# First norm over GpSimd's products, silus one turn later, and the delta rule five ticks earlier

## The chip, the cores and the metric

The kernel runs on one core of one Trainium2 chip, whose engines work side by side: TensorE (PE, with PEld for its weight loads), VectorE (DVE), ScalarE (ACT), GpSimd (POOL) and SyncE (SP), which issues the loads. The metric is the device time of one execution in microseconds (us). Less is better.

## The reference, cut to what matters

Two transformer blocks run one after the other on 512 tokens of width 1024. The change lies in the first block, from its start to the end of its input projection.

```python
c_act = jax.nn.silu(c)
mod = (c_act @ w_ada[l] + b_ada[l])[:, None, :]
shift1, scale1, gate1, shift2, scale2, gate2 = jnp.split(mod, 6, axis=-1)
h = rms_norm(x, norm1_w[l]) * (1.0 + scale1) + shift1
# in hybrid_mixer(h, ...)
p = h @ w_in
qkv = jax.nn.silu(causal_depthwise_conv(p[..., Q_OFF:Z_OFF], conv_qkv_w))
...
o = gated_delta_rule_chunked(l2_normalize(q), l2_normalize(k), v, g, beta)
```

The delta rule takes 64 tokens at a time: from q, k, v and the decays it inverts a triangular 64x64 matrix for each chunk and head, and then carries a 128x128 state for each head from chunk to chunk.

## The kernel before

Everything is held with the features on the 128 partitions: X is 8 tiles of 128x512 (KT = 8). Each engine has a program of its own (`tensor`, `vector`, `scalar`, `gpsimd`, `sync`). The order on an engine is the order in which its Python function is written, and semaphores join the engines.

**The norm.** ScalarE squares X tile by tile (L1679), GpSimd adds six of the squares (L2186), TensorE sums over the partitions with a matrix of ones (`sum_squares`, L518 and L521), and ScalarE makes the reciprocal root RSTD by Ln and Exp (`rstd`, L1694 and L1696). Meanwhile the first two of the six parts of the modulation (shift1 and scale1) are formed from 16 slabs of w_ada in the buffer ADA: of each part TensorE multiplies two slabs (`ada_direct`, L542) and VectorE weighs and adds six (`weigh`, L1053 and L1056), which TensorE then sums (`ada_column`, L533). `apply_norm` (L1082, L1075) on VectorE and `upper` (L1721) on ScalarE write the normed X as a high part HH and a low part HL.

**The matmuls.** Each weight slab of 128x1024 is loaded into one of four buffers RAWS (L2350). ScalarE rounds it into WH (`split_to`, L1666), GpSimd forms the rest WL in four pieces of 128x256 (L2169), and TensorE multiplies in eight k steps of three matmuls each (`slab_gemm`, L498). There are three WH and three WL, so WH of a slab waits for the matmul of the slab three before. `begin(which, j, 1)` splits up to one slab beyond the named one. The first slab, `ab` (512 wide, for the decays), runs in alternation with the first slab of w_in. I call the slabs of w_in w0 to w27, in their order.

**Slabs w0 to w11** are q, k and v. They end in one of two PSUM banks, in turn. ScalarE reads a bank twice (`evict`: STG at L1745, TMP at L1747), VectorE adds three taps of the convolution (`convolve`, L1140), and ScalarE applies the silu (`silu`, L1752), for q and k also the square (L1755). TensorE sums the squares of four heads at a time (`l2_sums`, L572), ScalarE forms the roots (`l2_roots`, L1761 and L1764), and VectorE scales the heads (`unit_heads`, L1147). Between them VectorE weighs one further slab of w_ada per turn. The loads of w_in and of w_ada alternate in one queue of SyncE: a w_ada slab waits for the buffer that VectorE's weighing two w_ada slabs earlier frees, and the w_in slab behind it in the queue waits with it.

**Slabs w10 to w27 and the delta rule** are woven: each engine alternates the stream `project_rest` (two ticks, and again two) with the stream of the delta rule (two ticks, and then three). A k step of TensorE is one tick, a slab is eight. The delta stream begins after DELTA_TICKS empty ticks. In it two prepared pairs of chunks and one scan take turns. `prepare` begins with two broadcasts of the decays and of beta (L680, L684, 8 matmuls each in the profile), then k and q products, transposes (kq, tr) and the inversion (L615, L634); `scan` carries the state (L738 to L751).

## Time and profile before

| | us |
|---|---|
| median of 3 runs | 2103.99 (2103.61 to 2108.41) |
| profiled execution | 2104.05 |
| its span | 2102.8 |
| PE busy | 1945.7 (93%) |
| PEld busy | 1657.3 (79%) |
| DVE busy | 680.6 (32%) |
| ACT busy | 710.3 (34%) |
| POOL busy | 950.0 (45%) |
| mean granted clock | 0.963 |

The table is of the whole span. The change touches the first 385 us only, so the shares of busy time say little; what counts there is where TensorE stands still, which instruction ends each wait, and which clock it was granted. Busy times of TensorE are modelled, since matmuls are pipelined: a matmul of 128x512 starts 0.23 us after the one before at the higher clock. The row that the timeline gives after idle time names the engine and line that released it; "issue" stands where the profile shows no releaser, and then the semaphore that the program waits on has to be found in the other engines' rows.

### The profile page before, as it was taken

The page shows a single profiled execution, that of the slowest core. Times are in us where ns is not written, and L with a number is a line of the kernel's source. Part 1 is how long each engine was busy: PE and PEld are TensorE (multiplying, and loading weights), DVE is VectorE, ACT ScalarE, POOL GpSimd, SP SyncE. Part 2 cuts the span into 40 slices and gives each one's busy share as a digit, 9 for nine tenths or more (in the row PEclk, how much of TensorE's full clock was granted, in tenths as well). Part 3 has the DMA queues.
Part 4 walks back from the last instruction along what each step waited for, and adds up shares of the span by engine and source line. Part 5 has one row for each costly group of instructions (what it writes and reads, how often), then busy time and mean ns, then how long its engine had stood idle before and what let it go on. Part 6 is the DMA issues. An engine that isn't in the chain of part 4 may idle for free.

```text
span 2102.8 us, 32887 instructions
## 1 busy us (share of the span) xinstructions
PE 1945.7 (93%) x13928; PEld 1657.3 (79%) x13928; DVE 680.6 (32%) x1069; ACT 710.3 (34%) x1093; POOL 950.0 (45%) x1257
## 2 busy tenths in 40 slices
PE   5879989999999999999999999977777799999997
PEld 4657767777788889999999989966666478888885
DVE  6554452232111102232210055654454522222101
ACT  3573221332232234222222243444455343222222
POOL 3442231535545566555555455421122166555564
PEclk8999998999999999999999999998999899999998
DMA  7332121324332233222222422100000323322231
GB/s 279 120 123 98 68 94 32 102 73 146 120 101 88 90 96 97 91 91 91 89 83 94 131 88 86 45 7 2 2 2 2 130 80 101 92 99 91 92 101 58
DMA packets 54690, 182.75 MB, mean 87 GB/s; under 512 B 6512, under 2 KB 6768, under 8 KB 54416
## 3 DMA queue, kind: packets, MB, share of 16 engines
q1 hardware_dynamic: 54544, 180.65, 26.1%
q8 instruction: 110, 1.80, 0.3%
q14 instruction: 36, 0.29, 0.0%
HBM read 175.39 MB, written 5.24 MB: 86 GB/s over the span
## 4 chain that ended last, share of the span: by engine, by line
PE 81%; DVE 7%; ACT 6%; DMA 3%; issue 2%; POOL 1%; SPq 1%; DVEq 0%; ACTq 0%
PE PS L498 67%; PE PS L615 3%; PE PS L969 1%; DVE TMP L1140 1%; DMA ADA<-w_ada 1%; PE PS L962 1%; POOL WL L2169 1%; ACT WH L1666 1%; PE PS L976 1%; PE PS L987 1%; DMA BON<-bsave 1%; DMA RAWS<-w_f0g 1%; ACT L1673 0%; PE PS L744 0%; PE PS L748 0%
## 5 line engine op out<-in xcount | busy, mean ns | idle before, releaser
L2169 POOL TENSOR_TENSOR WL<-RAWS,WH 128x256 fp32r<-128x256 f32 x1074 | 822.2, 797 | 809.8 <-ACT WH L1666 809.7
L498 PE MATMUL PS<-HH,WH 128*128 128x264 f32 (+2 forms) x2184 | 670.7, 349 | 47.3 <-issue 10.6
L498 PE MATMUL PS<-HL,WH 128*128 128x264 f32 (+2 forms) x2184 | 656.1, 342 | 0.0
L498 PE MATMUL PS<-HH,WL 128*128 128x264 f32 (+2 forms) x2184 | 654.1, 341 | 0.0
L498 PEld LDWEIGHTS PS<-HH,WH 128*128 128x128 f32 (+1 forms) x2184 | 378.3, 191 | 114.8 <-issue 31.5
L1666 ACT ACTIVATE WH<-RAWS 128x1024 fp32r<-128x1024 f32 (+2 forms) x275 | 283.7, 1033 | 457.5 <-PE PS L498 401.9
L498 PEld LDWEIGHTS PS<-HH,WL 128*128 128x128 f32 (+1 forms) x2184 | 378.8, 191 | 48.8 <-issue 0.6
L498 PEld LDWEIGHTS PS<-HL,WH 128*128 128x128 f32 (+1 forms) x2184 | 379.0, 190 | 48.0 <-issue 2.6
L498 PE MATMUL PS<-IHf,WH 128*128 128x512 f32 (+1 forms) x704 | 209.4, 338 | 0.0
L498 PE MATMUL PS<-IHf,WL 128*128 128x512 f32 (+1 forms) x704 | 209.2, 338 | 0.0
L498 PE MATMUL PS<-ILf,WH 128*128 128x512 f32 (+1 forms) x704 | 209.2, 338 | 0.0
L1401 DVE TENSOR_TENSOR TMP<-TMP,PS 128x512 f32<-128x512 f32 (+1 forms) x66 | 45.8, 693 | 322.9 <-PE PS L498 308.0
L1944 ACT ACTIVATE IHf<-TMP 128x512 fp32r<-128x512 f32 (+1 forms) x66 | 42.0, 636 | 286.5 <-DVE TMP L1401 286.5
L498 PEld LDWEIGHTS PS<-IHf,WH 128*128 128x128 f32 x704 | 120.6, 188 | 14.9
L498 PEld LDWEIGHTS PS<-ILf,WH 128*128 128x128 f32 x704 | 120.7, 188 | 14.7
L498 PEld LDWEIGHTS PS<-IHf,WL 128*128 128x128 f32 x704 | 120.4, 188 | 14.9
L1408 DVE SCALAR_TENSOR_TENSOR X<-PS,X 128x528 f32<-128x528 f32 (+1 forms) x16 | 11.2, 700 | 222.5 <-PE PS L498 222.5
L2186 POOL TENSOR_TENSOR SQA<-SQA,TMP 128x512 f32<-128x512 f32 (+1 forms) x39 | 53.1, 1363 | 63.2 <-ACT TMP L1679 62.5
L1389 DVE TENSOR_TENSOR TMP<-PS,RSTD 128x528 f32<-128x528 f32 (+1 forms) x44 | 30.8, 700 | 151.1 <-PE PS L498 150.4
L1403 DVE TENSOR_TENSOR ILf<-TMP,IHf 128x512 fp32r<-128x512 f32 (+1 forms) x66 | 46.8, 709 | 46.4 <-ACT IHf L1944 46.4
L1679 ACT ACTIVATE TMP<-X 128x512 f32<-128x512 f32 (+1 forms) x42 | 26.1, 626 | 85.8 <-DVE X L1408 35.7
L1396 DVE TENSOR_TENSOR TMP<-TMP,RSTD 128x528 f32<-128x528 f32 (+1 forms) x44 | 36.7, 833 | 41.3 <-ACT TMP L1940 41.3
(498 smaller groups left out, 1810.7 us busy)
## 6 DMA issues: line engine op xcount, KB each, us to landing
RAWS<-w_w_in SPq DMA_DIRECT2D x52, 512.0 KB, 4.3
RAWS<-w_ada SPq DMA_DIRECT2D x32, 512.0 KB, 3.6
RAWS<-w_f0g SPq DMA_DIRECT2D x22, 512.0 KB, 3.5
RAWS<-w_f0u SPq DMA_DIRECT2D x22, 512.0 KB, 3.6
RAWS<-w_f1g SPq DMA_DIRECT2D x22, 512.0 KB, 3.5
RAWS<-w_f1u SPq DMA_DIRECT2D x22, 512.0 KB, 3.5
RAWS<-w_f2g SPq DMA_DIRECT2D x22, 512.0 KB, 3.5
RAWS<-w_f2u SPq DMA_DIRECT2D x22, 512.0 KB, 3.5
```

Of the source, the lines that this page charges most:

```text
L498: ins = te.matmul(ps[0:m, q, o:o + b - a] if len(halves) > 1 else ps[0:m, o:o + b - a], w[:, k * m:k * m + m], v[:, k0 + k, a:b], start=fi ...
L615: ins = te.matmul(h4(b[:, 0:256])[q, u, :], lhs[q, u, :], con("ident")[q, q] if rhs is None else rhs[q, u, :], start=True, stop=True)
L962: te.matmul(PS[:, b, 0:n], KA[q, i, 128 * j:128 * j + 128], QA[q, i, 512 - n:512], start=True, stop=True).then_inc(*hp[b].up("z", r))
L1389: ve.tensor_tensor(tv, place(f, 2 * j), r, ALU.mult).then_inc(*ff_g.up("g", FT * (f - 1) + j))
L1396: ve.tensor_tensor(tv, tv, r, ALU.mult).then_inc(*ff_g.up("r", FT * (f - 1) + j))
L1401: ve.tensor_tensor(tv, tv, place(f, 2 * j + 1), ALU.mult).then_inc(*ff_mul.up(FT * f + j))
L1403: ve.tensor_tensor(IL[f][:, j, :], t, IH[f][:, j, :].bitcast(f32), ALU.subtract).then_inc(*ff_lo.up(FT * f + j))
L1666: ae.activation(WH[s % NS][:, 0:n], RAW[i % NR][:, 0:n], ACT.Copy).then_inc(*w_hi.up(s))
L1679: ae.activation((TMP[k % 3] if k else SQA)[:, 0:n], X[:, k, t0:T2], ACT.Square).then_inc(*n_sq.up(8 * SQUARED[q] + k))
L1944: ae.activation(IH[f][:, j, :], t, ACT.Copy).then_inc(*ff_hi.up(FT * f + j))
L2169: ins = ge.tensor_tensor(WL[s % NS][:, p], RAW[i % NR][:, p], WH[s % NS][:, p].bitcast(f32), ALU.subtract)
L2186: ge.tensor_tensor(SQA[:, 0:n], SQA[:, 0:n], TMP[k % 3][:, 0:n], ALU.add).then_inc(*n_acc.up(added(q, k)[1] - 1))
```

## The change

It has three parts.

1. GpSimd multiplies each tile of X by RSTD into a new buffer XRS, which lies behind ADA in memory that later tensors use. ScalarE forms HH from XRS in one instruction with scale SC and shift MOD, and VectorE forms the same value in TMP with `tensor_scalar` and subtracts HH. On TensorE the sum of squares moves between the two `ada_direct`. On GpSimd the memset of ST, which lies over XRS, moves behind the splits of w0 to w11 and waits for the last HL.
2. On ScalarE `silu(i - 1)` in the turn of slab i becomes `silu(i - 2)`, and so on to slab 12, where `log_and_exp` (which loads the table with Exp and Ln) now follows silu(11).
3. DELTA_TICKS goes from 30 to 25 on all four engines.

```diff
-DELTA_TICKS = 30
+DELTA_TICKS = 25
...
         te.wait_ge(*c_act.at("silu"))
-        for v in range(2):
-            ada_direct(v, bank(v))
+        ada_direct(0, bank(0))
         te.wait_ge(s_k0, 16)
         sum_squares(0)
+        ada_direct(1, bank(1))
...
-        apply_norm(0, SC[:, 0:8], MOD[:, 0:8], NM)
+        def first_low(k):
+            ve.wait_ge(*n_h.at(k))
+            ve.wait_ge(*n_hi.at(k))
+            ve.tensor_tensor(HL[:, k, NM:T2], TMP[k % 3][:, 0:T1], HH[:, k, NM:T2].bitcast(f32),
+                             ALU.subtract).then_inc(*n_lo.up(k))
+
+        for k in range(KT):
+            ve.wait_ge(*n_xr.at(k))
+            if k >= 3:
+                ve.wait_ge(*n_lo.at(k - 3))
+            ve.tensor_scalar(TMP[k % 3][:, 0:T1], XR[k], SC[:, k:k + 1], MOD[:, k:k + 1], ALU.mult,
+                             ALU.add).then_inc(*n_h.up(k))
+            if k:
+                first_low(k - 1)
+        first_low(KT - 1)
...
-        upper(0, MOD[:, 0:8], NM)
+        ae.wait_ge(*s_sc.at(0))
+        for k in range(KT):
+            ae.wait_ge(*n_xr.at(k))
+            ae.activation(HH[:, k, NM:T2], XR[k], ACT.Identity, bias=MOD[:, k:k + 1],
+                          scale=SC[:, k:k + 1]).then_inc(*n_hi.up(k))
...
-            silu(i - 1)
+            if i > 1:
+                silu(i - 2)
...
         evict(9)
+        silu(8)
         begin("w_in", IN_ORDER[11], 1)
         l2_roots(4)
-        silu(9)
...
-                if 10 < i < 13:
-                    silu(i - 1)
                 for _ in range(8):
                     yield
                 if i < 12:
                     evict(i)
+                    silu(i - 1)
                     continue
...
+                    if i == 12:
+                        silu(11)
+                        log_and_exp()
...
         pr, dr = project_rest(), later_by(DELTA_TICKS, pipeline(4, prepare, scan))
-        log_and_exp()
...
+        ge.wait_ge(*n_rs.at("r0"))
+        for k in range(KT):
+            ge.tensor_tensor(XR[k], X[:, k, NM:T2], RSTD[:, 0:T1], ALU.mult).then_inc(*n_xr.up(k))
         ge.wait_ge(*ada_col.at(1))
         for i in range(2):
             ge.memset(STG[i][:, 0:3], 0.0).then_inc(*zeros.up(f"stg{i}"))
         ge.memset(ROW[:, :], 0.0).then_inc(*zeros.up("row"))
+        begin("w_in", IN_ORDER[10], 1)
+        ge.wait_ge(*n_lo.at(7))
         ge.memset(ST[:, :, :], 0.0).then_inc(*zeros.up("st"))
-        begin("w_in", IN_ORDER[10], 1)
```

GpSimd's queue at the start, before: the additions of squares, memsets, and the WL pieces.

```order
7 L2186 TENSOR_TENSOR SQA<-SQA,TMP 128x512 x6
8 L2194 MEMSET STG 128x3 x2
9 L2195 MEMSET ROW 64x512
10 L2196 MEMSET ST 128x512
11 L2169 TENSOR_TENSOR WL<-RAWS,WH 128x256 x66
```

GpSimd's queue at the start, after:

```order
7 L2210 TENSOR_TENSOR SQA<-SQA,TMP 128x512 x6
8 L2218 TENSOR_TENSOR XRS<-X,RSTD 128x512 x8
9 L2221 MEMSET STG 128x3 x2
10 L2222 MEMSET ROW 64x512
11 L2193 TENSOR_TENSOR WL<-RAWS,WH 128x256 x50
12 L2225 MEMSET ST 128x512
```

Eight products stand ahead of the memsets and of every WL piece, and the memset of ST stands behind 50 pieces.

ScalarE's queue after the roots of heads 4 to 7 (X<-X), up to the first instruction of the delta rule (L1861 before, L1886 after), before:

```order
76 L1764 ACTIVATE X<-X 128x512 x4
77 L1752 ACT_TABLE_LOAD
78 L1752 ACTIVATE QKV<-TMP 128x512
79 L1673 ACT_TABLE_LOAD
80 L1745 ACTIVATE STG<-PS 128x512
81 L1747 ACTIVATE TMP<-PS,CV 128x512
82 L1752 ACT_TABLE_LOAD
83 L1752 ACTIVATE QKV<-TMP 128x512
84 L1745 ACTIVATE STG<-PS 128x512
85 L1747 ACTIVATE TMP<-PS,CV 128x512
86 L1666 ACTIVATE WH<-RAWS 128x1024
87 L1752 ACTIVATE QKV<-TMP 128x512
```

and after:

```order
76 L1786 ACTIVATE X<-X 128x512 x4
77 L1767 ACTIVATE STG<-PS 128x512
78 L1769 ACTIVATE TMP<-PS,CV 128x512
79 L1774 ACT_TABLE_LOAD
80 L1774 ACTIVATE QKV<-TMP 128x512
81 L1767 ACTIVATE STG<-PS 128x512
82 L1769 ACTIVATE TMP<-PS,CV 128x512
83 L1774 ACTIVATE QKV<-TMP 128x512
84 L1684 ACTIVATE WH<-RAWS 128x1024
85 L1886 ACT_TABLE_LOAD
86 L1886 ACTIVATE X<-PS 128x512
87 L1830 ACTIVATE Z<-PS 128x512
```

The eviction of w10 (STG, TMP) stands directly behind the roots, and EG of the delta rule (X<-PS) stands ahead of the eviction of w12 (Z).

TensorE's queue around the second broadcasts of the delta rule, before (w13, k steps 2 and 3 between the two):

```order
350 L680 MATMUL PS<-ROW,KC 128x128 x4
351 L684 MATMUL PS<-ROW,KC 128x128 x4
352 L498 MATMUL PS<-HH,WH 128x512
353 L498 MATMUL PS<-HL,WH 128x512
354 L498 MATMUL PS<-HH,WL 128x512
355 L498 MATMUL PS<-HH,WH 128x512
356 L498 MATMUL PS<-HL,WH 128x512
357 L498 MATMUL PS<-HH,WL 128x512
358 L680 MATMUL PS<-ROW,KC 128x128 x4
359 L684 MATMUL PS<-ROW,KC 128x128 x4
```

and after (w12, k steps 6 and 7 between the two):

```order
339 L684 MATMUL PS<-ROW,KC 128x128 x4
340 L688 MATMUL PS<-ROW,KC 128x128 x4
341 L502 MATMUL PS<-HH,WH 128x512
342 L502 MATMUL PS<-HL,WH 128x512
343 L502 MATMUL PS<-HH,WL 128x512
344 L502 MATMUL PS<-HH,WH 128x512
345 L502 MATMUL PS<-HL,WH 128x512
346 L502 MATMUL PS<-HH,WL 128x512
347 L684 MATMUL PS<-ROW,KC 128x128 x4
348 L688 MATMUL PS<-ROW,KC 128x128 x4
```

The broadcasts moved ahead by four k steps, 12 matmuls of the projection.

## Rows read from the trace of the kernel before

**Rows 1.** The page, part 2: tenths in 40 slices of 52.6 us.
```profile
PE   5879989999999999999999999977777799999997
...
PEclk8999998999999999999999999998999899999998
```

**Rows 2.** Timeline, 18 to 46 us: start, duration, engine, line, tiles, count, idle before.
```profile
18.06 6.87 DVE L1056 SCALAR_TENSOR_TENSOR ACC<-ADA,CA,ACC 128x1024 f32<-128x1024 f32 x4 [1.79 <-DMA ADA<-w_ada]
...
23.20 6.99 PE L542 MATMUL PS<-CA,ADA 128*128 128x1 f32 x32 [1.42 <-DMA ADA<-w_ada]
...
28.30 5.53 DVE L1056 SCALAR_TENSOR_TENSOR ACC<-ADA,CA,ACC 128x1024 f32<-128x1024 f32 x4 [0.39 <-DMA ADA<-w_ada]
...
33.77 0.69 ACT L1694 ACTIVATE RSTD<-PS,EPSC 128x512 f32<-128x512 f32 x1 [14.22 <-PE PS L521]
...
34.49 0.63 ACT L1696 ACTIVATE RSTD<-RSTD 128x512 f32<-128x512 f32 x1
...
44.83 0.80 PE L498 MATMUL PS<-HH,WH 128*128 128x512 f32 x1 [2.39 <-POOL WL L2169]
```

**Rows 3.** Timeline of GpSimd, additions, memsets and WL pieces.
```profile
10.83 10.18 POOL L2186 TENSOR_TENSOR SQA<-SQA,TMP 128x512 f32<-128x512 f32 x6 [9.94 <-ACT TMP L1679]
...
37.38 0.14 POOL L2194 MEMSET STG<- 128x3 f32 x2 [16.37 <-PE PS L533]
...
38.38 6.39 POOL L2169 TENSOR_TENSOR WL<-RAWS,WH 128x256 fp32r<-128x256 f32 x6
```

**Rows 4.** Timeline of TensorE, projection: instructions after idle time.
```profile
60.61 0.57 PE L498 MATMUL PS<-HH,WH 128*128 128x512 f32 x1 [2.46 <-issue]
...
75.60 0.47 PE L498 MATMUL PS<-HH,WH 128*128 128x512 f32 x1 [1.64 <-issue]
...
82.22 0.47 PE L498 MATMUL PS<-HH,WH 128*128 128x512 f32 x1 [0.83 <-issue]
...
120.69 0.79 PE L498 MATMUL PS<-HH,WH 128*128 128x512 f32 x1 [4.63 <-ACT TMP L1747]
...
147.31 0.50 PE L498 MATMUL PS<-HH,WH 128*128 128x512 f32 x1 [2.13 <-ACT TMP L1747]
...
157.23 0.76 PE L498 MATMUL PS<-HH,WH 128*128 128x512 f32 x1 [4.05 <-issue]
```

**Rows 5.** Tile SQA, 10 to 30 us: ns shortest, median, longest.
```profile
L2186 POOL TENSOR_TENSOR SQA<-SQA,TMP x6: 1262/1398/2065, 10.8 to 18.9; 128x512 f32<-128x512 f32 x6
```

**Rows 6.** Timeline of ScalarE and the load queue: turns of the loop.
```profile
77.28 1.04 ACT L1666 ACTIVATE WH<-RAWS 128x1024 fp32r<-128x1024 f32 x1
...
82.69 0.63 ACT L1752 ACTIVATE QKV<-TMP 128x512 f32<-128x512 f32 x1 [3.31 <-DVE TMP L1140]
...
83.90 1.04 ACT L1666 ACTIVATE WH<-RAWS 128x1024 fp32r<-128x1024 f32 x1
...
105.65 0.43 SPq L2350 DMA_DIRECT2D RAWS<-w_w_in  x1
...
110.11 1.06 ACT L1666 ACTIVATE WH<-RAWS 128x1024 fp32r<-128x1024 f32 x1 [2.71 <-DMA RAWS<-w_w_in]
```

**Rows 7.** Windows of TensorE: us, busy (instructions), granted clock, DMA share, GB/s.
```profile
83.00:87.60 4.60, 4.60 (x21) 1.00 0.46 154
...
160.00:165.00 5.00, 5.00 (x20) 0.50 0.10 38
...
352.00:376.00 24.00, 22.44 (x84) 0.57 0.13 43
```

**Rows 8.** Timeline of ScalarE after the two groups of roots.
```profile
119.48 0.58 ACT L1745 ACTIVATE STG<-PS 128x512 f32<-128x512 f32 x1
...
144.79 1.28 ACT L1673 ACT_TABLE_LOAD   x1
```

**Rows 9.** Timeline of TensorE in the delta rule.
```profile
167.62 1.05 PE L684 MATMUL PS<-ROW,KC 64*128 64x128 f32 x8
...
301.62 0.68 PE L615 MATMUL PS<-iv1LD,iv1UD 64*64 64x64 f32 x16 [2.93 <-DVE iv1LD L1234]
```

More of the change, by code:

```diff
@@ L203, in program @@
     ADA = sbuf("ADA", [128, 16, SLAB], st=m0)
+    XRS = sbuf("XRS", [128, KT * T1], st=m0)
     m0.close()
@@ L330, in program @@
     n_res, n_pre, n_outp = count("n_res"), count("n_pre"), count("n_outp")
+    n_xr = count("n_xr")
     ff_silu, ff_mul, ff_hi, ff_lo, ff_x = (count(x) for x in ("ff_silu", "ff_mul", "ff_hi", "ff_lo", "ff_x"))
@@ L446, in place @@
         return pair((job + 2) % 3) if f == 1 else bank(job % 6)
+    XR = [XRS[:, 512 * k:512 * k + 512] for k in range(KT)]
     NORMED = {0: 0, 1: 1, 3: 2, 4: 3, 5: 4}
```

## The prediction

> **What bounds the kernel now.** I read the page's 40 slices first [rows 1]: TensorE is busy 9 tenths nearly everywhere until 1425 us, but not in the first three slices (0 to 158 us). Between TensorE's instructions the kernel is nearly saturated, so a gain can only come from time in which TensorE stands still or runs at the lower of its two clocks (0.50 granted is 1.2 GHz, 1.00 is 2.4 GHz). All three parts of the change lie before 385 us, where the input projection ends. There the timeline shows where TensorE stood: for the conditioning at the start [rows 2], for GpSimd's low halves of the weights [rows 3], and at eight places in the projection, of which six stand in [rows 4]. Everything after 385 us follows in order and should only slide. The profiled execution took 2104.05 us (span 2102.8), the median of the three runs is 2103.99, so I count from 2104.05.
>
> **Part 1, the start.** Before, TensorE waits 1.42 us for the second half of w_ada, multiplies until 30.2, sums the squares until 33.7, and ends the columns at 37.3, which releases GpSimd [rows 2, 3]. After, the sums of squares (3.7 us) stand between the two halves: 21.8 to 25.5; the second half runs to 32.5 and the first eight columns to 34.4, with no idle time. The reciprocal root, 0.69 + 0.63 us on ScalarE, is ready at 26.9 instead of 35.1 [rows 2]. That alone would end the columns 1.1 us sooner.
>
> But the first projection's pair of slabs does not wait for the norm: its first matmul at 44.83 is released by GpSimd's WL [rows 2], and from there TensorE has no other wait until 60.61 [rows 4], so none for a norm tile. The bound is GpSimd's queue: memsets from 37.4, then six WL pieces in 6.39 us [rows 3]. The change puts eight products of 128x512 ahead of those. No row has them there. The nearest are the six additions of the same size: shortest 1.26, longest 2.07 us, six in 10.18 [rows 3, 5]. They are long where VectorE works beside them, and VectorE is then slowed too: four weighings take 6.87 us with GpSimd busy for the first half, 5.53 with it idle [rows 2].
> The Trainium skill has a rule that speaks against this edit (SBUF — State Buffer, section Who interferes with whom): a VectorE instruction with two SBUF inputs contends with a GpSimd instruction that reads SBUF, and one of them blocks for the whole of the other. Taken to the letter a product beside a weighing would cost 1.26 + 1.28 = 2.5 us and the pair would start near 53, for a sum of 2095. The longest row, 2.07, has not shown that much.
>
> I take 1.87 us for a product while VectorE is busy and 1.3 otherwise. VectorE's last four weighings then take 4 x 1.9 from 28.3, until 35.9; by then 4.8 products are done. The second eight columns wait for that weighing: 36.0 to 37.8, SC at 38.1. By then 6.5 products are done; the rest takes 2.7 us beside VectorE, to 40.9. Memsets 0.6 (the one of ST, 0.5, is moved away) and six WL at 1.1 give 48.1. So the pair starts **3.3 us later** than at 44.83. Bounds: all products at 1.26 from 26.95 on and WL as before, -0.4 us; all at 2.07 and WL at 1.14, +6.1. VectorE's and ScalarE's cheaper norm (the products are taken from them) is worth nothing here, since HL was not waited for. The clock is low at the pair's start in both kernels, since TensorE stands still before it in both.
>
> **Part 2, the silus, slabs 1 to 9.** One turn of ScalarE's loop is WH at 77.28, two evictions, a wait of 3.3 us for VectorE's three taps, silu and square, WH at 83.90: 6.62 us [rows 6]. Then WL takes 3.7 and TensorE starts: idle 0.83 at 82.22 (three such places) and 1.64 at 75.60 [rows 4]. A slab needs only 24 x 0.23 = 5.55 us (20 starts in 4.6 us; the row counts one more, under way [rows 7]). With silu(i-2) the wait for taps is gone. What is late next is the DMA: the load of w(n+3) is queued behind an ada slab that waits for VectorE's weighing of slab n, itself behind the taps; issued at 105.65 it lets ScalarE start at 110.11, 4.45 us later [rows 6]. I walk it on, in the times of before (evictions 1.15, taps 3.2, weighing 1.3, WH 1.05, WL done 3.85 after it). WH of w3 67.0, WL done 71.9: w3 starts at 73.96, idle 0. Load of w4 lands at 75.5, WL done 80.4: w4 at 80.45. Then w5 86.0, the l2 sums 91.6 to 95.3, w6 95.3, w7 100.85, w8 106.4.
> The roots: the load of w9 lands at 103.6 (before: 110.11); WH, table, four Ln, four Exp, silu, square are 9.4 us from WH's start to the next eviction at 119.48 [rows 6, 8], plus 1.15: 114.2. So **w9 starts at 114.2 instead of 120.69**, after 2.2 us idle instead of 4.63 [rows 4], and I take it that it then stays at 2.4 GHz (a wait of 2.13 at 147.31 left it there; one of 2.46 at 60.61 did not). If it falls, 12 matmuls x 0.2 = 2.4 us come back; I charge half, 1.2.
>
> **Part 3, slabs 10 to 13.** w10 waits for the eviction of w9, which stands behind WH of w11, whose load waits for VectorE after the w9 start (taps, unit heads, weighing, landing: 11 us): 127.0 instead of 133.5. w12 waits for the eviction of w10. Before, this one stood behind two table loads of 1.28 and a silu of 0.63 after the roots, 3.3 us with the gaps, the last ending at 146.07 [rows 6, 8]; after, it stands directly behind the roots. WH of w12 at 129.1 makes the roots end at 136.0 and the eviction at 137.15, before w11 ends at 138.1. **w12 starts at 138.1, not 147.31.** Inside w12 now stand the first broadcasts of the delta rule, 2.2 us at 2.4 GHz. The second ones end at 148.05. w13's load lands at 143.1 and its WL at 148.0: no idle time, where before there were 4.05 us and after them the lower clock (0.50 from 160 to 165) [rows 4, 7]. One common point: both broadcasts and four steps of w13 done. Before this is 168.7 (the second broadcasts end at 167.62 + 1.05 [rows 9]); after, 148.05 + 4 x 3 x 0.23 = 150.8. **That is 17.9 us sooner**, start excluded.
> The added table loads (Exp for EG inside w12, Silu and back for silu(11)) put WH of w14 at 149.9 and its WL at 154; TensorE has work until 160.9. They cost nothing; without the two kq pieces and the transposes, 7.2 us, as cover they would.
>
> **Part 4, the weaving itself.** The delta rule stands four k steps, 2.8 us, earlier in TensorE's order from there on, and 12 projection matmuls more follow its last sum. Busy work is equal, so only waits and clock count. Before has single waits for VectorE, the longest 2.93 us at 301.62 [rows 9], where the short convolution sits in VectorE's queue, and 24 us at the end with a clock of 0.57 [rows 7], which is 22.44 x 0.43 = 9.6 us of lost work. The shift redraws them and nothing says which way: I take 0, bounds -8 (most of the slow end and one wait gone) to +8 (as much again). Of the end, the wait of 0.20 for the last gated part goes; the 1.60 for the short convolution stays.
>
> **The sum.** +3.3 - 17.9 + 1.2 - 0.2 + 0 = -13.6, so 2104.05 - 13.6 = **2090.5 us**.
>
> **Rivals.** (a) *The start is free and the delta stretch falls well.* VectorE's weighing does not hold GpSimd back: -0.4 instead of +3.3, and the slow end shrinks by 5: about 2082. For it: the shortest addition took 1.26; against: four of six were far longer. (b) *The loads bind.* My walk leaves w4 to w9 within 1 us of the DMA. If each landing is 1 us later (the 4.45 is one row), the evictions of w7 and w9 come 3 us later each, and a fall of the clock at w9 and w13 costs 2.4 + 3.7: with that the gain is 13.6 - 9 = 4.5: 2099.5. (c) *The silus move nothing*: something else, such as the evictions of TMP for a later slab, holds TensorE as before; then only w12's 3.3 us and w13's wait stay, less the start: 2104 - 4 = 2100 or more, counted as the same. Against it: each of these waits ends in a WL or an eviction that I traced to ScalarE's queue. (d) *Slower*: the delta rule in its new place meets VectorE's taps so that TensorE stays at 1.2 GHz through it. It would have to lose 13.6 + 6.3 = 20 us, which is 40 us more at the lower clock in the 215 us after w13; before has some 24 at the end. It decides from a third wait of over 2 us in each of the two delta pairs. That gives 2112.
>
> **Chances.** The forecast with its bounds (2084 to 2097) 0.62, (a) 0.14, (b) 0.13, (c) 0.07, (d) 0.04. The range from 2080 to 2100 takes in the forecast, most of (a) and (b). A measurement can tell about 0.3% from no change, 6.3 us. Faster than 2097.7: 0.62 + 0.14 + a third of (b) + 0.05 of redrawn waits from the rest = 0.85; within 0.3%: 0.12; slower: 0.03.
>
> **What would show it.** The profile after should have: eight GpSimd products from 27 us with a mean near 1.7 us, and the pair's start near 48 released by WL; no wait of TensorE between 60 and 95 us over 1 us; w9's wait near 2 us, w12's gone, w13's gone, with the broadcasts at 2.4 GHz; the second broadcasts some 14 us sooner than at 168.7. The step that I trust least is part 4, then GpSimd's products. I am wrong if the loads arrive later than walked (ScalarE's WH then waits for DMA in most turns), or if TensorE's clock falls at w9.

## The result, and the profile after

| | before | after |
|---|---|---|
| median | 2104.82 us (2101.99 to 2108.41, 6 runs) | 2090.17 us (2086.21 to 2097.61, 6 runs) |
| profiled execution, its span | 2104.05, 2102.8 | 2090.22, 2089.0 |
| PE busy | 1945.7 | 1938.2 |
| mean granted clock | 0.963 | 0.964 |

The ratio is 0.9937, with a 95% interval from 0.992 to 0.9954. The change is faster by 0.6%, and 2090.5 had been forecast. The sum came out within 1 us, but several of its terms were off and cancelled, so much of that agreement is luck.

The page after, part 2, answers to [rows 1]: TensorE's first slice is emptier, the second and third are fuller.

```profile
PE   4999998999999999999999899977777799999997
...
PEclk7999999999999999999999999998989899999998
```

**The start.** The timeline of the changed kernel between 25 and 65 us. The columns are start, duration, engine, line, operation, tiles, shapes, count, and idle time before with what ended it.

```profile
25.80 4.08 PE L546 MATMUL PS<-CA,ADA 128*128 128x1 f32 x32
...
27.47 14.64 POOL L2218 TENSOR_TENSOR XRS<-X,RSTD 128x512 f32<-128x512 f32 x8 [5.85 <-ACT RSTD L1714]
...
28.88 8.44 DVE L1060 SCALAR_TENSOR_TENSOR ACC<-ADA,CA,ACC 128x1024 f32<-128x1024 f32 x4 [0.39 <-DMA ADA<-w_ada]
...
37.37 3.58 PE L537 MATMUL PS<-KC,ACC 128*128 128x1 f32 x16 [4.43 <-DVE ACC L1060]
...
42.17 5.30 DVE L1144 TENSOR_SCALAR TMP<-XRS,SC,MOD 128x512 f32<-128x512 f32 x2
...
42.60 4.13 POOL L2193 TENSOR_TENSOR WL<-RAWS,WH 128x256 fp32r<-128x256 f32 x6
...
48.22 0.66 PE L502 MATMUL PS<-HH,WH 128*64 128x512 f32 x1 [7.28 <-DVE HL L1137]
...
49.53 0.63 PE L502 MATMUL PS<-HH,WH 128*128 128x512 f32 x1
...
64.66 0.77 PE L502 MATMUL PS<-HH,WH 128*128 128x512 f32 x1 [2.46 <-issue]
```

The pair of slabs starts at 48.22, released by HL and not by GpSimd's WL as was walked. That it reads like the forecast of 48.1 is chance: 48.22 is the first matmul of `ab` (128*64), and 48.1 was counted from 44.83, the first matmul of w0 (128*128) in the kernel before. There `ab` had started at 40.94, and it waited for HL as well:

```profile
40.94 0.66 PE L498 MATMUL PS<-HH,WH 128*64 128x512 f32 x1 [3.63 <-DVE HL L1075]
```

Like for like, `ab` starts 7.3 us later, w0 4.7 (49.53 against 44.83) and w1 4.05 (64.66 against 60.61). From here on I give the start of w0 or of w1 where kernels with and without part 1 are compared. The six WL took 4.13 us instead of the 6.6 in the sum, and VectorE's first two `tensor_scalar` took 5.30 us together. The tile's own list shows that this is one instruction, 4849 ns long, while the median is 536 ns. It also shows the products: median 2192 ns beside VectorE, above the 1.87 us assumed and above the bound of 2.07.

```profile
L2218 POOL TENSOR_TENSOR XRS<-X,RSTD x8: 1262/2192/2247, 27.5 to 40.8; 128x512 f32<-128x512 f32 x8
...
L1144 DVE TENSOR_SCALAR TMP<-XRS,SC,MOD x8: 534/536/4849, 42.2 to 55.2; 128x512 f32<-128x512 f32 x8
```

**The middle.** Some of TensorE's instructions after idle time and the last broadcasts, with two of ScalarE's rows between them. They answer to [rows 4, 6, 9].

```profile
80.40 1.06 ACT L1684 ACTIVATE WH<-RAWS 128x1024 fp32r<-128x1024 f32 x1 [4.71 <-DMA RAWS<-w_w_in]
...
85.35 0.47 PE L502 MATMUL PS<-HH,WH 128*128 128x512 f32 x1 [1.78 <-issue]
...
119.84 0.80 PE L502 MATMUL PS<-HH,WH 128*128 128x512 f32 x1 [2.93 <-ACT TMP L1769]
...
132.49 1.06 ACT L1684 ACTIVATE WH<-RAWS 128x1024 fp32r<-128x1024 f32 x1 [8.33 <-DMA RAWS<-w_w_in]
...
134.66 0.50 PE L502 MATMUL PS<-HH,WH 128*128 128x512 f32 x1 [1.08 <-ACT TMP L1769]
...
154.81 1.05 PE L688 MATMUL PS<-ROW,KC 64*128 64x128 f32 x8
```

The waits ahead of w12 (2.13) and of w13 (4.05) are gone, and the broadcasts run at the higher clock. But ScalarE waits for a load in most turns, and w4 (85.35), w9 (119.84) and w10 (134.66) wait.

**The delta stretch.** Windows from the common point of the prediction (both broadcasts and four k steps of w13) to the end of the projection, where TensorE waits for the next norm: of before, then of after. The columns are length, busy time (instructions) of PE, PEld, DVE, ACT and POOL, granted clock, DMA share, GB/s.

```profile
168.60:427.28 258.68, 243.16 (x2057) 191.76 (x2056) 103.35 (x200) 68.35 (x115) 84.49 (x106) 0.95 0.24 80
```

```profile
158.70:409.00 250.30, 237.64 (x2057) 187.25 (x2055) 102.14 (x192) 68.17 (x116) 89.31 (x110) 0.97 0.25 83
```

The same 2057 matmuls stand in both. After, the stretch is 8.4 us shorter: 5.5 us less busy time at a higher clock, and 2.9 us less idle time (12.7 instead of 15.5). The longest waits in it, before and then after, were these (total, times, longest):

```profile
PE PS L615 <- DVE iv0LD L1234: 3.2, 2, 2.3
PE PS L615 <- DVE iv1LD L1234: 2.9, 1, 2.9
```

```profile
PE PS L502 <- DVE HL L1241: 2.8, 1, 2.8
PE PS L718 <- DVE XX L1286: 2.1, 4, 0.5
```

The inversion's two waits of over 2 us for VectorE [rows 9] have left; what TensorE now waits for longest is the low half of the short convolution's result (HL from YS, L1241).

**The account.** Four points of every traced execution, in us: the start of w1, the common point, the start of the slab after the next norm (f0), and from there to the end of the span. Each is read from the timeline of TensorE.

| trace | w1 | common point | to f0 | f0 to end | span |
|---|---|---|---|---|---|
| before | 60.61 | 168.6 | 262.7 | 1671.5 | 2102.8 |
| before_again | 63.38 | 173.4 | 263.9 | 1674.5 | 2111.8 |
| norm_only | 62.75 | 168.1 | 266.5 | 1678.2 | 2112.8 |
| silus_only | 63.08 | 160.3 | 259.2 | 1674.6 | 2094.1 |
| weave_only | 60.71 | 160.2 | 251.3 | 1674.2 | 2085.7 |
| norm_undone | 63.27 | 158.5 | 257.5 | 1678.2 | 2094.2 |
| norm_undone_2 | 63.09 | 158.4 | 251.1 | 1677.5 | 2087.0 |
| after | 64.66 | 158.7 | 254.4 | 1675.9 | 2089.0 |
| after_again | 63.80 | 159.5 | 250.5 | 1674.5 | 2084.5 |
| norm_one_form | 63.64 | 158.1 | 256.3 | 1675.1 | 2089.5 |
| norm_low_waits | 64.19 | 157.7 | 253.7 | 1674.5 | 2085.9 |
| norm_second_memset | 63.58 | 159.1 | 256.2 | 1671.8 | 2087.1 |
| low_halves_first | 56.76 | 152.3 | 250.3 | 1671.1 | 2073.7 |
| low_halves_first_2 | 56.80 | 152.3 | 256.3 | 1675.2 | 2083.8 |

From f0 on all kernels have the same code, and it takes between 1671.1 and 1678.2 us. That is the noise in which 7 us of any one trace are lost; a term below that is better read from the points than from the whole time. In the profiled pair the gain is 9.9 us up to the common point and 8.3 from there to f0; 4.4 are lost again behind it, where nothing was changed: 13.8 in all.

### The profile page after: what moved, and what is told of

It reads as the page before. It is cut to its first block, busy times and chain, and to the rows that moved or that the text cites. A ratio compares the mean times of both kernels' runs of the same rounds, so it can differ in the third digit from the quotient of the medians.

```text
span 2089.0 us, 32909 instructions
## 1 busy us (share of the span) xinstructions
PE 1938.2 (93%) x13928; PEld 1652.6 (79%) x13928; DVE 689.6 (33%) x1069; ACT 710.4 (34%) x1093; POOL 966.4 (46%) x1265
## 4 chain that ended last, share of the span: by engine, by line
PE 81%; DVE 7%; ACT 5%; DMA 4%; issue 2%; SPq 1%; POOL 1%; DVEq 0%; ACTq 0%
PE PS L502 68%; PE PS L619 3%; PE PS L973 1%; DMA ADA<-w_ada 1%; DMA RAWS<-w_w_in 1%; PE PS L966 1%; PE PS L980 1%; DVE ACC L1060 1%; PE PS L991 1%; DMA BON<-bsave 1%; DMA RAWS<-w_f0g 1%; ACT WH L1684 0%; DVE HL L1603 0%; PE PS L947 0%; PE PS L638 0%
## 5 line engine op out<-in xcount | busy, mean ns | idle before, releaser
L502 PEld LDWEIGHTS PS<-HL,WH 128*128 128x128 f32 (+1 forms) x2184 | 378.8, 190 | 48.1 <-issue 2.4
L502 PEld LDWEIGHTS PS<-ILf,WH 128*128 128x128 f32 x704 | 120.6, 188 | 14.7
```

Source lines behind the costliest of these rows:

```text
L502: ins = te.matmul(ps[0:m, q, o:o + b - a] if len(halves) > 1 else ps[0:m, o:o + b - a], w[:, k * m:k * m + m], v[:, k0 + k, a:b], start=fi ...
```

## Experiments

### One part at a time

**norm_only** is part 1 alone: GpSimd's eight products and the sum of squares moved.

```diff
-        for v in range(2):
-            ada_direct(v, bank(v))
+        ada_direct(0, bank(0))
         te.wait_ge(s_k0, 16)
         sum_squares(0)
+        ada_direct(1, bank(1))
...
+        for k in range(KT):
+            ge.tensor_tensor(XR[k], X[:, k, NM:T2], RSTD[:, 0:T1], ALU.mult).then_inc(*n_xr.up(k))
```

> The kernel before with part 1 alone (the norm over GpSimd's products, the sum of squares between the two direct products). Theory: the start is longer, and the rest slides by it. TensorE's first full pair of matmuls starts near 48.2 us instead of 44.8, behind GpSimd's products (14.6 us) and VectorE's first low tile, so the kernel is 3 to 4 us slower than before: near 2108. Rival, the start is free: same as before within 1 us, 2104. Rival, the edit gains by itself: 2100 or less.

Measured: 2109.98 us (2102.85 to 2114.7, 6 runs), ratio 1.0027 (1.0009 to 1.0045), beside 2103.99 for before. Part 1 alone makes the kernel slower. The trace does not show the way that the theory gives, though (a longer start, and the rest slides by it): w1 starts 2.1 us later than in before, but the common point is at 168.1, against 168.6 in before and 173.4 in before_again. What this trace loses lies behind that point, where part 1 changed nothing (the moved memset runs at 137.84), so what the 6 us of the medians come from is not shown. `ab` starts at 47.72, and again HL releases it:

```profile
25.27 6.83 PE L546 MATMUL PS<-CA,ADA 128*128 128x1 f32 x32
...
47.72 0.66 PE L502 MATMUL PS<-HH,WH 128*64 128x512 f32 x1 [7.28 <-DVE HL L1137]
```

**silus_only** is part 2 alone: `silu(i - 2)` in the turn of slab i.

```diff
-            silu(i - 1)
+            if i > 1:
+                silu(i - 2)
...
+                    if i == 12:
+                        silu(11)
+                        log_and_exp()
```

> The kernel before with part 2 alone (each silu one turn later). Theory: this part carries nearly all of the gain. The waits of TensorE at 75.6, 82.2 and 88.8 us go, the one of slab w9 falls from 4.6 to about 2.5 us, those of w12 and w13 shrink by 2 and 3; the second broadcasts of the delta rule end 13 to 17 us sooner than at 168.7, and the time is 2088 to 2094. Rival, parts 2 and 3 are worth about the same: 2097 or more.

Measured: 2095.59 us (2094.18 to 2097.07, 4 runs), ratio 0.996 (0.9945 to 0.9974). This is 8.4 us, over half of the whole gain but not nearly all of it. Its trace has waits where that of after has them (w4, w9, w10), so these come with the silus and not with the norm; w10 waits 3.66 us, and w13 (the last row) still 1.78:

```profile
83.65 0.47 PE L498 MATMUL PS<-HH,WH 128*128 128x512 f32 x1 [2.06 <-issue]
...
118.03 0.50 PE L498 MATMUL PS<-HH,WH 128*128 128x512 f32 x1 [2.85 <-ACT TMP L1747]
...
132.78 0.50 PE L498 MATMUL PS<-HH,WH 128*128 128x512 f32 x1 [3.66 <-ACT TMP L1747]
...
153.16 0.47 PE L498 MATMUL PS<-HH,WH 128*128 128x512 f32 x1 [1.78 <-issue]
```

**weave_only** is part 3 alone.

```diff
-DELTA_TICKS = 30
+DELTA_TICKS = 25
```

> The kernel before with part 3 alone (the delta rule 25 ticks late instead of 30). Theory: busy work is equal, the first broadcasts now fill part of the waits before w13, so 1 to 4 us are gained there, and waits and clock in the delta stretch are redrawn by some us: 2098 to 2104. In the profile the last sum of the delta rule stands some 2.8 us of projection work further from w_out. Rival: the slow end (granted clock 0.57 from 352 to 376 us before) goes with this part alone and it gives 8 us or more: 2096 or less.

Measured: 2093.65 us (2086.95 to 2094.65, 4 runs), ratio 0.9952 (0.9935 to 0.9968). The theory (2098 to 2104) fell and its rival of 8 us or more holds: one number is worth as much as the whole rewriting of ScalarE's queue. Its wait ahead of w12 is 2.06 us, where before has 2.13; the wait ahead of w13 has gone, since the first broadcasts lie ahead of it, and the stretch up to f0 is 11.4 us shorter than that of before:

```profile
147.33 0.50 PE L498 MATMUL PS<-HH,WH 128*128 128x512 f32 x1 [2.06 <-ACT TMP L1747]
...
156.27 1.05 PE L684 MATMUL PS<-ROW,KC 64*128 64x128 f32 x8
...
160.20:407.50 247.30, 234.34 (x2057) 184.53 (x2055) 103.15 (x195) 67.46 (x112) 88.94 (x110) 0.99 0.26 84
```

**norm_undone** is parts 2 and 3 without part 1; it ran a second time (norm_undone_2) beside a version below.

> The changed kernel with part 1 undone (parts 2 and 3 together on the start of before). Theory: the start is 3.5 to 4 us shorter than in the changed kernel and nothing else changes, so it is faster than the changed kernel by 2 to 4 us: 2086 to 2088. Rival, the later start costs nothing, since the loads of the weights give the pace after it: same as the changed kernel, 2090.

> Parts 2 and 3 alone once more, next to the version with the low halves first, in one call, since 2085.9 (4 runs, 2079.8 to 2095.5) and 2083.5 (6 runs, 2075.0 to 2090.7) don't tell the two apart. If a sooner start is worth its time to the end, this one is 4 to 6 us slower than the other (2086 to 2088 against 2081 to 2083): in its trace w1 begins 3 to 6 us later than at 56.76. If the start is paid back in the projection's waits for loads or in the clock, both give 2084.

Measured: 2085.94 us (2079.82 to 2095.48, 4 runs), ratio 0.9918 (0.9887 to 0.9948), and 2087.18 us (2080.09 to 2095.53, 6 runs), ratio 0.99 (0.988 to 0.992). The median of all ten is 2087.2, that of seven runs of the changed kernel 2090.1. The ratios, each to runs of the kernel before that were taken beside it, are 0.9918 and 0.99 against 0.9937. So part 1 gives nothing and may cost some 3 us inside the change too; that it costs is not shown, since the ranges overlap, and at the common point the difference is small: 158.5 and 158.4 against 158.7 and 159.5.

By medians the parts alone give +6.0, -8.4 and -10.3, in sum -12.7, and together -14.7. Up to the common point they do not add, though: with w1 subtracted, silus_only is 10.8 ahead of before (97.2 instead of 108.0), weave_only 8.5, and both together (norm_undone) 12.8, since both parts remove the wait of w13 and the low clock behind it.

### Is the later start a matter of the execution?

In silus_only and norm_undone w0 started 3.3 us later than in before, with the same code up to there. The 32 column matmuls of 128x1 took 6.83 us, not 3.74. So both kernels of the comparison ran once more unchanged, for their traces.

> The kernel before once more, for its trace. In the kernel with part 2 alone and in that with parts 2 and 3 the 32 columns at the start took 6.83 us, in the kernel before and in that with part 3 alone 3.74, though this code is the same in all four and the records give the granted clock as 1.00 in all four; the pair started 3.3 us later there. My theory: this is a matter of the execution, not of the kernel (TensorE is near a change of its clock there), so the kernel before will sometimes have it too: either 3.7 or 6.8 us here, nothing between. Rival: the kernels differ by it, then this one has 3.74 again.

> The changed kernel once more, for its trace. There the second direct product took 4.08 us (6.99 before), the first eight columns 3.20 and the last eight 3.58 us; in the kernel with part 1 alone 6.83, 3.55 and 3.58. My theory: as in the run of the kernel before, each of these stretches has either some 0.11 or some 0.21 us for a column and which one changes between executions; the columns end near 41 in any case, because the second half waits for VectorE's weighing until 37.4; so the pair starts within 0.7 us of 48.2, released by HL, and GpSimd's six WL take 4.1 us while VectorE's first two tensor_scalar take 5.3. Rival: the split (WL undisturbed, tensor_scalar held off) is chance too, and here the WL take 6 us and the tensor_scalar 2.

Measured, before_again (2113.01 us, one run):

```profile
33.56 6.83 PE L533 MATMUL PS<-KC,ACC 128*128 128x1 f32 x32
...
47.90 0.79 PE L498 MATMUL PS<-HH,WH 128*128 128x512 f32 x1 [2.38 <-POOL WL L2169]
...
63.38 0.77 PE L498 MATMUL PS<-HH,WH 128*128 128x512 f32 x1 [2.46 <-issue]
```

And after_again (2085.71 us, one run):

```profile
25.29 3.71 PE L546 MATMUL PS<-CA,ADA 128*128 128x1 f32 x32
...
28.86 3.56 PE L537 MATMUL PS<-KC,ACC 128*128 128x1 f32 x16
...
36.88 3.57 PE L537 MATMUL PS<-KC,ACC 128*128 128x1 f32 x16 [4.46 <-DVE ACC L1060]
...
47.74 0.66 PE L502 MATMUL PS<-HH,WH 128*64 128x512 f32 x1 [7.29 <-DVE HL L1137]
```

The first theory stands: the kernel before has both kinds of start. A column is two matmuls of 128x1 in the profile. With the sums behind both direct products (six traces), the 32 matmuls take 3.7 us twice and 6.8 four times, with nothing between. With the sums ahead of the second direct product (eight traces), that product takes 3.7 to 4.1 five times and 6.83 three times; the first eight columns (16 matmuls) behind it take 3.55 us in all but one (3.20), and the last eight 3.57 or 3.58 us in all eight. The part that may run fast is thus the 3 to 4 us behind the sums; part 1 moved it from the columns, which everything waits for, to a product that ends long before VectorE's last weighing.

The prediction compared with a trace of the quick kind, where w0 starts at 44.83 and w1 at 60.61. At w1, the four traces with part 1 and GpSimd's queue as in the change (after, after_again, norm_only and norm_one_form below, 62.75 to 64.66) lie 3.0 us on average behind the quick kind (60.61, 60.71), but only 0.5 behind the slow kind (63.08 to 63.38). The other theory of after_again, that GpSimd's undisturbed WL and the held `tensor_scalar` were chance, falls: WL 4.13 us and 5.31 us for the two again.

### What holds VectorE at the first HL

**norm_one_form** writes the `tensor_scalar` as the form that before used, with two tensor operands.

```diff
-            ve.tensor_scalar(TMP[k % 3][:, 0:T1], XR[k], SC[:, k:k + 1], MOD[:, k:k + 1], ALU.mult,
-                             ALU.add).then_inc(*n_h.up(k))
+            ve.scalar_tensor_tensor(TMP[k % 3][:, 0:T1], XR[k], SC[:, k:k + 1],
+                                    MOD[:, k:k + 1].broadcast_to([128, T1]), ALU.mult,
+                                    ALU.add).then_inc(*n_h.up(k))
```

> The changed kernel with VectorE's eight tensor_scalar of the first norm (line 1144: products times SC plus MOD, one tensor operand) written as scalar_tensor_tensor with MOD spread over the columns as a second tensor operand. In the changed kernel the first two took 5.30 us, exactly while GpSimd made six WL in 4.13 us (0.69 each), and the pair waited for HL until 48.22. My theory: the tensor_scalar is the instruction that GpSimd's queue holds off; written as the form which the kernel before used there, it shares: the first two take some 2 to 2.5 us, the first HL is ready near 44.5, and GpSimd's six WL take some 6 us again as before (6.39), so the pair starts near 47.5 to 48.5, now released by WL. Rival: it is the products' order or the buffers, not the form: then the first two again take 5.3 us and WL 4.1 us.

Measured: 2090.72 us (one run). The theory fell; the form does not matter:

```profile
41.72 5.78 DVE L1144 SCALAR_TENSOR_TENSOR TMP<-XRS,SC,MOD 128x512 f32<-128x512 f32 x2
...
42.15 4.14 POOL L2194 TENSOR_TENSOR WL<-RAWS,WH 128x256 fp32r<-128x256 f32 x6
```

**norm_low_waits** lets GpSimd begin its WL only when the first TMP is done.

```diff
         ge.memset(ROW[:, :], 0.0).then_inc(*zeros.up("row"))
+        ge.wait_ge(*n_h.at(0))
         begin("w_in", IN_ORDER[10], 1)
```

> The changed kernel with one wait more: GpSimd begins its six WL only after VectorE's first TMP (line 1144) is done. In all three traces with part 1 in which that was looked at, this one instruction takes 4.85 to 5.1 us, from 0.4 us before the first WL until 0.3 to 0.6 after the sixth, and each WL 0.72, while in the kernel before the two engines take turns (WL 1.17, VectorE 1.21). My theory: the VectorE instruction that is under way when GpSimd's row of WL begins is held until the row is over, and later ones share; with the wait the first TMP takes 0.54, is done at 42.7, and the engines take turns: each WL 1.0 to 1.2, the first HL ready at 44 instead of 47.4, the slab ab starts when its own WL is done, near 45, and w0 near 49, released by WL. Rival: GpSimd's WL hold whatever VectorE does for as long as they last; then the first TMP takes 0.54, but the second or the first HL takes some 4 us, WL 0.72, and the slab ab starts at 48 again.

Measured: 2087.14 us (one run). The first TMP is no longer held, the engines now take turns, at 0.9 to 1.2 us each, and `ab` starts 3.2 us sooner than in after_again:

```profile
41.57 1.20 DVE L1144 TENSOR_SCALAR TMP<-XRS,SC,MOD 128x512 f32<-128x512 f32 x2
...
42.40 10.10 POOL L2193 TENSOR_TENSOR WL<-RAWS,WH 128x256 fp32r<-128x256 f32 x10 [0.36 <-DVE TMP L1144]
...
44.53 0.69 PE L502 MATMUL PS<-HH,WH 128*64 128x512 f32 x1 [4.18 <-POOL WL L2193]
...
48.54 0.79 PE L502 MATMUL PS<-HH,WH 128*128 128x512 f32 x1 [2.46 <-POOL WL L2193]
```

The two TMP in the first of these rows, in ns (shortest, median, longest): the first took 747; the second, which was under way when the WL began at 42.40, took 528.

```profile
L1144 DVE TENSOR_SCALAR TMP<-XRS,SC,MOD x2: 528/638/747, 41.6 to 42.2; 128x512 f32<-128x512 f32 x2
```

Nothing is won by it: w0 cannot start before 48.54, since its own WL now come slower, and w1 starts at 64.19.

**norm_second_memset** puts a second memset of ROW ahead of the WL, so that the first TMP would meet memsets alone.

```diff
+        ge.memset(ROW[:, :], 0.0).then_inc(*zeros.up("row0"))
+        ge.wait_ge(*zeros.at("row0"))
         ge.memset(ROW[:, :], 0.0).then_inc(*zeros.up("row"))
         begin("w_in", IN_ORDER[10], 1)
```

> The changed kernel with one memset of ROW more (0.52 us) between GpSimd's memsets and its WL, which puts 1.0 us of memsets between the end of the columns and the first WL, as in the kernel before (there ROW and ST). My theory: memsets do not hold VectorE (in the kernel before the first TMP took 0.74 beside them); the first TMP, 0.54 us, then ends before the first WL begins, and the two engines take turns as in the kernel before: WL 1.0 to 1.2 each, first HL near 44.2, w0 near 49. Rival: VectorE is held by the products or by what it reads (XRS), not by where its instruction meets the row of WL; then the first TMP takes 5.4 us again and the slab ab starts near 48.5.

Measured: 2088.32 us (one run). What was expected came half true. The first TMP met memsets alone, took 0.55 us and was done before the first WL began. But the two engines did not take turns then: now the second TMP, which began at 42.31 beside the second memset, was held across the six WL, for 4.93 us, and the pair started at 47.99, as late as in after_again (47.74). The second memset took 0.74 instead of 0.52 us.

```profile
41.85 5.39 DVE L1144 TENSOR_SCALAR TMP<-XRS,SC,MOD 128x512 f32<-128x512 f32 x2
...
42.12 0.74 POOL L2224 MEMSET ROW<- 64x512 f32 x1
```

```profile
L1144 DVE TENSOR_SCALAR TMP<-XRS,SC,MOD x2: 546/2738/4930, 41.9 to 42.3; 128x512 f32<-128x512 f32 x2
```

What the runs show is this. In all five traces one VectorE instruction was held until GpSimd's row ended, whatever its form and whichever TMP it was, and the later ones shared. In each of them the held instruction had begun while GpSimd's last memset ahead of the WL was under way, with no gap before the WL (42.17 in after, the memset from 42.11 to 42.63). "Under way when the row begins" is not enough: the second TMP of norm_low_waits was that, after a gap of 0.36 us, and took 528 ns, while the first WL took 950 ns instead of 720. In the kernel before, whose row has no gap either, VectorE had nothing that began beside the last memset: its first TMP began at 37.75 and took 752 ns, the memset of ST ran from 37.90, and its second TMP began at 38.42, just behind the first WL (38.38); from there the two take turns [rows 3]. No run tests this feature by itself, so why the instruction is held stays open. The Trainium skill (SBUF — State Buffer, section Who interferes with whom) says that of two contending instructions the later one blocks for the whole of the other. The held instruction agrees in kind, but it was held through six others in a row, which that rule does not say; and beside the products the two engines took turns at 2.2 and 2.1 us, less than the 2.5 that the prediction worked out by the rule.

### The low halves first

The experiments say: the norm's products give nothing, and before the change w0 waits for GpSimd's WL, which need only the weights. **low_halves_first** has parts 2 and 3 and the earlier sum of squares; VectorE keeps its norm, and GpSimd makes the WL of `ab` and w0 while it would wait for the conditioning.

```diff
         add_squares(0, T1, *range(1, 7))
+        begin("ab", 0, 1)
         ge.wait_ge(*ada_col.at(1))
         for i in range(2):
             ge.memset(STG[i][:, 0:3], 0.0).then_inc(*zeros.up(f"stg{i}"))
```

> Parts 2 and 3 as in the changed kernel. Of part 1 only the earlier sum of squares is kept (it stands between the two direct products); the eight products with RSTD stay with VectorE, and in their place GpSimd makes the low halves WL of the slab ab and of w0 while it would otherwise wait for the conditioning, so that they stand ahead of its wait and of its memsets. My theory: in the kernel before the pair of slabs starts when these WL are done, 7.5 us after the columns end (37.3 to 44.83), and VectorE's first HL is ready 3.5 us after the columns; so with WL done early the slab ab starts about 3.6 us after the last column and w0 some 1.3 us after it, that is near 41 us if the 32 columns take 3.7 us, near 44 if they take 6.8 as in the run without part 1; the run is then 3 to 4 us below the kernel with parts 2 and 3 alone (2085.9 median) and 7 below the changed kernel, 2082 to 2083. Rival: the start does not matter, since w1 waits for its load anyway (before: 2.46 us idle at 60.61); then the pair starts sooner but w1 starts at the same time as before and the run gives 2086.

> The version with the low halves of ab and w0 ahead of the conditioning once more, beside parts 2 and 3 alone. The columns at the start take 3.9 and 3.6 us for eight and eight of the slow kind or half of that, by the execution, so the slab ab starts between 37.5 and 41 and w1 between 53 and 57. Sooner start worth its time: 2081 to 2083, 4 to 6 us under parts 2 and 3 alone. Paid back: 2084 to 2086, the same as those.

Measured: 2083.5 us (2074.95 to 2090.7, 6 runs), ratio 0.9907 (0.9887 to 0.9928), and when it ran again 2078.7 us (2072.81 to 2085.04, 5 runs), ratio 0.9855 (0.9834 to 0.9876), where parts 2 and 3 alone, run beside it, had 2087.18 (0.99, 0.988 to 0.992). Over all their runs the medians are 2082.0 (11 runs) and 2087.2 (10 runs).

```profile
32.45 5.15 POOL L2171 TENSOR_TENSOR WL<-RAWS,WH 128x256 fp32r<-128x256 f32 x6 [11.21 <-ACT WH L1666]
...
34.34 3.57 PE L533 MATMUL PS<-KC,ACC 128*128 128x1 f32 x16 [1.82 <-DVE ACC L1056]
...
40.80 0.66 PE L498 MATMUL PS<-HH,WH 128*64 128x512 f32 x1 [2.88 <-DVE HL L1075]
...
56.76 0.47 PE L498 MATMUL PS<-HH,WH 128*128 128x512 f32 x1 [2.46 <-issue]
```

The six WL lie beside the weighings, and the columns end at 38 us; the pair starts with `ab` at 40.80 and runs through, and w1 starts at 56.76, 6.4 us sooner than in norm_undone. The common point keeps 6.1 of these (152.3 against 158.4). This version beats both kernels: some 8 us under the changed one by the medians. Both traces of norm_undone have the slow columns, though. Against the quick kind (before) `ab` starts no sooner (40.80 against 40.94), and what is left is w0 without its wait of 2.39 us for WL, and w1 3.9 us sooner (56.76 against 60.61). Which of the two edits (WL first, or the sum of squares between the products) brings how much was not separated; against the slow kind the columns' end moved by some 2.6 us.

## Why the prediction was right, and where it was not

1. **The start, +3.3 us** (measured: +4.7 at w0, +4.05 at w1, of which 0.6 is a load that landed later). The number came near by errors of opposite sign. Failed: *"HL was not waited for"*. In the kernel before, `ab` already waited 3.63 us for HL, and HL released the pair in every trace with part 1 in which GpSimd did not wait for VectorE. Failed: the columns' end, forecast 37.8 and measured 40.95, since the last eight columns took 3.58 us and not 1.8, and the weighings ended at 37.3 and not 35.9. Mis-sized: the products, 2.19 us beside VectorE (forecast 1.87), and WL, 0.69 each (forecast 1.1). And the trace that it was counted from had the quick kind of columns: with before_again instead, w1 starts 1.3 us later in after and 0.4 in after_again.
2. **The middle, -17.9 + 1.2** (measured: -9.9 at the common point; without the start, -13.9). The mechanism was right and the size 2.8 us too large. The step that failed is the walk of the loads: w4's WH began at 80.40 after a load, where the walk had 75.5 + 3.3 = 78.8, and w4 started at 85.35, not 83.75. w9 started at 119.84 (walked: 114.2 + 3.3 = 117.5) after 2.93 us. The largest miss is w10, at 134.66 instead of 127.0 + 3.3 = 130.3: from w9's start to WH of w11 the walk charged 11 us, and it took 12.65 (119.84 to 132.49), in after_again 12.7. This is rival (b) in a small dose. The charge of 1.2 for the clock stood for nothing: the granted clock over 118 to 124 us was 0.57 in after and 1.00 in after_again, but from w9 to w10 both took the same, 14.82 and 14.87 us, because w10 waits for the eviction behind that load and not for TensorE.
3. **w12 and w13** were right: no wait at either, and the broadcasts at 1.16 and 1.05 us, the higher clock, instead of 2.07 and 1.91 for the first ones before.
4. **The weaving, 0 with bounds of 8**. This is the term that was mis-sized: from the common point to f0 the ten traces with part 3 take 250.3 to 257.4, the four without it 259.2 to 266.5. The means are 253.8 and 263.1, so it is worth some -9 us, the lower bound and a little more. The waits are the steady part: TensorE is idle for 12.1 to 13.0 us of the stretch with part 3 and for 15.4 to 18.0 without it, some 4 us, and the inversion's waits of 2.3 and 2.9 us are in all four without it and in none with it. The other 5 are clock (mean busy time 237 instead of 242), and they scatter: silus_only had 237.2 without part 3, and the same kernel 241.0 and 234.3 with it (norm_undone, norm_undone_2). Why the clock is higher with part 3 is not shown.
5. **Behind f0** 4.4 us were lost in the profiled pair. No part of the change reaches there, and the other traces show that stretch anywhere from 1671.1 to 1678.2. The forecast of -13.6 came true because this loss and the smaller middle stood against the gain of the weaving. That is luck.

The rivals: (a), a free start and a good delta stretch, was half right, in its second half. (b) came true by some 3 us. (c) and (d) fell: silus_only and weave_only each moved the time by 8 us or more, and the delta stretch ran at a clock of 0.95 to 0.99 in the ten traces with part 3. Both of the signs by which the prediction said that it would be wrong appeared in the profiled pair, loads that arrive later than walked (8 of ScalarE's 12 WH between 60 and 155 us wait for one, 3 of 11 before) and a lower clock at w9; the first cost 3 us, the second nothing.

## What to carry to other kernels

Before an edit of 3 us is priced against one trace, look whether a stretch of TensorE near it takes one of two lengths; a second trace of the same kernel showed here that most of what part 1 cost at the start was the luck of the first. Work that an idle engine can do early should be the work that the next stage waits for last (here the low halves of the weights), not work that only shortens another idle engine's part. And where a woven stream is placed by one number, that number deserves an experiment of its own: it was worth as much as a rewritten queue.

## What the runs showed of the hardware

**Columns at two speeds under one granted clock.** Windows of 33.5 to 37 us, with the columns running: of before, where 32 take 3.74 us, and of before_again, where they take 6.83 us. The clock column reads 0.99 and 1.00.

```profile
33.50:37.00 3.50, 3.50 (x33) 3.43 (x31) 0.50 (x2) 2.78 (x4) 0.00 (x0) 0.99 0.29 111
```

```profile
33.50:37.00 3.50, 3.50 (x18) 3.44 (x17) 0.28 (x1) 2.78 (x4) 0.00 (x0) 1.00 0.24 91
```

So a recorded clock of 1.00 does not say that matmuls run at the higher speed; their count per time does. The record is doubtful for the whole start. In before the second sum of squares (L521, from 31.89) took 1.84 us at a recorded 1.00, and that of the next norm, of the same form, 1.12:

```profile
426.16 1.12 PE L521 MATMUL PS<-TMP,KC 128*128 128x512 f32 x2 [0.65 <-ACT TMP L1679]
```

And in before_again the record stays at 1.00 while the matmuls of the pair start 0.43 us apart (48.49, 48.92), the distance that they have in before at a recorded 0.50 (45.43, 45.85). The simplest reading, an inference from these rows, is that the start runs at the lower clock in every trace, that in the quick kind the clock rises for the 3 to 4 us behind the sums, and that the record shows the level only from its first change on. Why it rises in some executions and not in others is not known.

**GpSimd's unbroken row.** Six WL in 4.13 us, and one VectorE instruction of 4.85 to 5.12 us beside them (usually 0.54 or 0.74, by its form), in all five traces of part 1 without a gap in the row. If TensorE waits for VectorE's first result, the wait is as long as GpSimd's row; if it waits for GpSimd, the row is finished sooner than when they share (4.13 instead of 6.39 us).
